# Sums of the normalised residual made one token tile at a time in a two-layer trunk kernel, and one sum for the down product made one place earlier

## What is computed

```python
def reference(x, norm_mix, w_in, sinks, w_s, b_s, w_o, norm_ffn, w_up, w_down, norm_final):
    for l in range(DEPTH):                      # DEPTH = 2
        h = rms_norm(x, norm_mix[l])
        proj = h @ w_in[l]
        ...                                     # att: windowed attention, sgu: spatial gating
        x = x + jnp.concatenate([att, sgu], axis=-1) @ w_o[l]
        h = rms_norm(x, norm_ffn[l])
        x = x + jnp.square(jax.nn.relu(h @ w_up[l])) @ w_down[l]
    return rms_norm(x, norm_final)
```

## Time and profile before

| | us |
|---|---|
| timed runs (3) | 948.45, 950.86, 953.03 |
| median | 950.86 |
| profiled execution: its own time | 949.33 |
| profiled execution: span of the trace | 947.4 |
| TensorE busy in the span | 930.3 (98%) |
| VectorE busy | 707.8 (75%) |
| ScalarE busy | 563.8 (60%) |
| GpSimd busy | 204.8 (22%) |
| mean granted TensorE clock, share of full speed | 0.994 |

### The profile page before, as it was taken

How to read it: one execution, slowest core, us unless ns; L and a number is a source line. 1 busy time by engine, 2 the same in 40 slices (tenths; PEclk the granted TensorE clock), 3 DMA queues, 4 the chain that set the end, 5 groups by cost and what they waited for, 6 DMA issues and landing times.

```text
span 947.4 us, 14055 instructions
## 1 busy us (share of the span) xinstructions
PE 930.3 (98%) x5632; PEld 819.0 (86%) x5632; DVE 707.8 (75%) x813; ACT 563.8 (60%) x843; POOL 204.8 (22%) x136
## 2 busy tenths in 40 slices
PE   8999999989999999999999999999899999999997
PEld 5888889978998998899888887899689989989985
DVE  5685525999779869879948752478987897798697
ACT  5556517775576376457655574377645756754764
POOL 2554224110011101011146433240101101101010
PEclk9999999999999999999999999999999999999999
DMA  9442150677668676676543320518668666676772
GB/s 292 127 135 71 42 150 28 167 166 206 147 171 204 134 232 134 178 190 156 165 150 134 112 68 23 155 24 245 139 173 205 149 198 158 161 198 150 205 156 89
DMA packets 40497, 141.76 MB, mean 150 GB/s; under 512 B 5616, under 2 KB 5744, under 8 KB 40432
## 3 DMA queue, kind: packets, MB, share of 16 engines
q1 hardware_dynamic: 28624, 98.32, 30.9%
q0 software_dynamic: 11520, 41.95, 25.3%
q10 hardware_dynamic: 288, 0.59, 0.2%
HBM read 138.74 MB, written 2.10 MB: 149 GB/s over the span
## 4 chain that ended last, share of the span: by engine, by line
PE 89%; DVE 6%; DMA 2%; ACT 1%; issue 1%; POOL 0%; DVEq 0%
PE bank L578 15%; PE bank L579 14%; PE bank L580 14%; PE bank L581 13%; PE bank L583 13%; PE bank L582 13%; DVE wlo L1316 2%; DMA raw<-weights_in 2%; PE bank L605 1%; PE bank L833 1%; PE bank L781 1%; DVE raw L1593 1%; PE bank L816 1%; PE bank L826 1%; PE bank L807 1%
## 5 line engine op out<-in xcount | busy, mean ns | idle before, releaser
L938 ACT ACTIVATE whi<-raw 128x1024 fp32r<-128x1024 f32 x268 | 281.0, 1057 | 165.2 <-PE bank L580 81.2
L1316 DVE TENSOR_TENSOR wlo<-raw,whi 128x1024 fp32r<-128x1024 f32 x218 | 264.8, 1223 | 79.8 <-ACT whi L938 79.4
L581 PE MATMUL bank<-xhi,wlo 128*128 128x256 f32 (+1 forms) x672 | 208.8, 311 | 0.0
L583 PE MATMUL bank<-xlo,whi 128*128 128x256 f32 (+1 forms) x672 | 207.3, 309 | 0.0
L582 PE MATMUL bank<-xhi,whi 128*128 128x256 f32 (+1 forms) x672 | 207.2, 308 | 0.0
L578 PE MATMUL bank<-wlo,fhi 128*128 128x512 f32 x448 | 176.3, 393 | 7.8 <-DVE flo L1580 7.8
L550 POOL DMA_DIRECT2D raw<-weights_in x80 | 69.4, 868 | 509.8 <-DVE raw L1593 236.0
L537 POOL TENSOR_TENSOR wlo<-raw,whi 128x1024 fp32r<-128x1024 f32 x50 | 135.2, 2714 | 195.4 <-ACT whi L938 195.4
L579 PE MATMUL bank<-whi,fhi 128*128 128x512 f32 x448 | 175.8, 392 | 0.0
L580 PE MATMUL bank<-whi,flo 128*128 128x512 f32 x448 | 175.5, 392 | 0.0
L581 PEld LDWEIGHTS bank<-xhi,wlo 128*128 128x128 f32 x672 | 128.3, 191 | 6.8 <-issue 0.3
(11 more groups left out here) (131 smaller groups left out, 1240.7 us busy)
## 6 DMA issues: line engine op xcount, KB each, us to landing
raw<-weights_in SPq DMA_DIRECT2D x172, 512.0 KB, 4.3
raw<-weights_in POOLq DMA_DIRECT2D x80, 512.0 KB, 6.1
xt<-x_in SPq DMA_DIRECT2D x4, 512.0 KB, 8.3
gbc<-gains_in SPq DMA_DIRECT2D x4, 512.0 KB, 4.3
out_t<-xt SPq DMA_DIRECT2D x3, 512.0 KB, 2.6
gbc<-gains_in ACTq DMA_DIRECT2D x1, 512.0 KB, 5.8
bias<-alibi_in SPq DMA_DIRECT2D x2, 256.0 KB, 7.3
wst<-ws_in SPq DMA_DIRECT2D x2, 256.0 KB, 7.0
```

The source lines that it names most:

```text
L581: pe.matmul(o, wlo[:, s, wc], hi[:, tokens], start=first, stop=False, skip_group_check=on_sum)
L583: return pe.matmul(o, whi[:, s, wc], lo[:, tokens], start=False, stop=last, skip_group_check=on_sum)
L938: act.activation(whi[:, n % SLOTS, :], raw_at(slot), ACT.Copy).then_inc(whi_ready, 1)
L1316: dve.tensor_tensor(wlo[:, n % SLOTS, :], raw_at(raw_slot(n)), whi[:, n % SLOTS, :], ALU.subtract) \
```

## The change

The four sums of the normalised residual are each made in two halves of 128 x 4 x 128, by tile pair. `made_x` counts the halves. The first half of S3 now stands between `turned_low` of tile 2 and `normed` of tile 3; the first halves of the other three stand between `normed` of tile 3 and `turned_low` of tile 3. The second halves stand where the whole sums stood. ScalarE waits for the second half of each. In the first quarter only, `make(q, 0)` moves ahead of the second low part of down's M1. The bodies of the sums are the same but for the token range.

```diff
+def made_x(l, i, k):
+    return l * 8 + 4 * k + i + 1
...
-                    made, src = ((1, s3), (3, xf[:, 0, :, :]), (2, xf[:, 3, :, :]), (4, xf[:, 1, :, :]))[i]
-                    act.wait_ge(xs_made, l * 4 + made)
+                    made, src = ((0, s3), (2, xf[:, 0, :, :]), (1, xf[:, 3, :, :]), (3, xf[:, 1, :, :]))[i]
+                    act.wait_ge(xs_made, made_x(l, made, 1))
...
+                def xs_make(i, k):
+                    x11, x12, x22, x21 = (xf[:, b, :, tok(k)] for b in range(4))
+                    if i == 0:
+                        dve.wait_ge(xf_ready, l * 2 * NT + 6 + 2 * k)
+                        dve.tensor_tensor(s3[:, :, tok(k)], x11, x21, ALU.subtract).then_inc(xs_made, 1)
+                    elif i == 1:
+                        dve.wait_ge(xs_made, made_x(l, 0, k))
+                        dve.tensor_tensor(x21, x22, x21, ALU.subtract).then_inc(xs_made, 1)
+                    elif i == 2:
+                        dve.wait_ge(xs_made, made_x(l, 1, k))
+                        dve.scalar_tensor_tensor(x11, x21, -1.0, x11, ALU.mult, ALU.subtract).then_inc(xs_made, 1)
+                    else:
+                        dve.wait_ge(xs_made, made_x(l, 2, k))
+                        dve.scalar_tensor_tensor(x12, x11, -1.0, x12, ALU.mult, ALU.subtract).then_inc(xs_made, 1)
...
                 for t in range(NT):
                     add(1, t)
                     if t:
                         turned_low(2 * l + 1, t - 1)
+                    if t == NT - 1:
+                        xs_make(0, 0)
                     normed(2 * l + 1, t)
+                for i in range(1, 4):
+                    xs_make(i, 0)
                 turned_low(2 * l + 1, NT - 1)
...
-                        xs_make(0)
+                        xs_make(0, 1)
                         low_up(q, M7, 0)
...
                         low_down(q, M1, 0)
+                        make(q, 0)
                         low_down(q, M1, 1)
                     else:
...
                         up_sum(q, M5, 1)
-                    make(q, 0)
+                        make(q, 0)
                     low_down(q, M7, 0)
```

More of the change, by code:

```diff
@@ L1626, in _ @@
                         low_up(q, M7, 1)
-                        xs_make(1)
-                        xs_make(2)
+                        xs_make(1, 1)
+                        xs_make(2, 1)
                         low_up(q, M6, 0)
@@ L1640, in _ @@
                         low_up(q, M5, 0)
-                        xs_make(3)
+                        xs_make(3, 1)
                         up_sum(q, M4, 0)
```

## The result

| | median, us | range, us | runs | profiled execution: own time, span |
|---|---|---|---|---|
| before | 951.23 | 948.45 to 953.03 | 7 | 949.33, 947.4 |
| after | 957.86 | 954.78 to 959.74 | 7 | 959.74, 957.9 |

The ratio of after to before is 1.0069 with a 95% interval of 1.0048 to 1.0089: the changed kernel is slower by 0.7%. That is 3.5 us above the forecast of 954.4, and 0.36 us outside the range.

A forecast was written before the change was run, and what follows sets the result against it. TensorE, busy 98%, was taken as the bound, with 11.2 us to win at its waits. 949.33 + 6.0 of new waits - 2.4 won = 952.9, plus 1.5 to the median: 954.4 us; 8-in-10 range 947.5 to 957.5.

The forecast's parts named there:

- The mechanism and place of the loss: Tile 3's norm: half sum and scaling wait for GpSimd on the shared SBUF port; TensorE waits 3.0 us a layer.
- that rival: Tile 3's norm: VectorE starts ahead of GpSimd; 951.7 us for both layers, about 953 for one; chance 0.25.
- The rival that the ports don't matter: Tile 3's norm: no turns with GpSimd, TensorE waits 2.4 us less; 948.5, or 945.1 with clock up; chance 0.18.
- The head start: VectorE behind tile 3: the first three halved sums save about 0.54 us each there, 1.6 us together.
- The gain ahead of M6: Down's first quarter: S3 fills VectorE's hole before M1's second low part; 2.4 us won in both layers.
- the upper end: Down's M1: its second weight block lands earlier, so the whole hole is won, 0.94 and 1.49 us.
- The lower end of the prediction: Down's M1: the block lands no earlier and ScalarE holds M7's low part; only 0.18 us won in layer 0.
- The argument on the queues: Ahead of M1's load: sums come 1.6 us earlier, accumulating transfers too, so queues are less full and the block lands earlier.
- Two falls in four places: TensorE's waits at M6 and tile 3's transposes, both layers: the clock falls twice, as many as before.
- The prediction's own figure for four falls: 957.8 us if the clock falls behind all four waits, at 1.7 us a fall.
- The slower rival: The clock falls behind the norm's new waits too, four falls at 1.7 us: 957 to 960 us; chance 0.12.

The follow-up runs named there:

- halves_only: The changed kernel with down's S3 back in its old place, so only the halved sums: 956.89 us, 1.0068 to before.
- psum_input: The changed kernel, but the half sum ahead of tile 3's scaling reads one input from PSUM instead of its SBUF copy: 951.16 us, 1.0009 to before.
- vector_first: The changed kernel, but GpSimd starts the low part of up's M2, second block, only after tile 3's scaling: 953.21 us, 1.0025 to before.
- halves_behind: The changed kernel with all four first half sums behind tile 3's scaling: 952.99 us, 1.002 to before.
- small_adds: Before with down's S3 moved and the first quarter's accumulating transfers for down's M7 cut to 64 of 1024 columns: 946.73 us, 0.996 to before.
- s3_turn: Before with down's S3 moved; first quarter's second accumulating transfer for down's M7 issued only after M1's second block landed: 947.83 us, 0.9956 to before.
- s3_only: The kernel before with only the move of down's S3 ahead of M1's second low part, first quarter: 951.68 us, 1.0005 to before.
- s3_turn_hidden: The kernel of `s3_turn` with ScalarE making M5's first hidden half ahead of the high part of M1's second block: 947.4 us, 0.995 to before.

## Why the prediction was right and wrong

**The mechanism and place of the loss: right.** The first half sum was forecast at 1.6 us and took 1.63 and 1.61. GpSimd was to be ahead by 0.04 and 0.02 us and was, by 0.05 and 0.01. The scaling was forecast at 3.5 (3.39 and 3.42), TensorE's waits at 3.0 (2.74 and 2.73). `halves_only` carries the whole loss; `psum_input` shows that the two inputs in SBUF are its condition; and `vector_first`, built so that VectorE wins the race, lands at 953.21 where that rival put 951.7 for both layers: its 1.6 us of waits came (1.3), but nothing was given back ahead of M6. The rival that the ports don't matter is out.

**The head start: right that it is small, and smaller still.** Where the half sums cost least (`halves_behind`), no gain from them is to be seen.

**The gain ahead of M6: wrong.** The step that failed is "I take the upper end: 0.94 + 1.49 = 2.4 us won". The block landed no earlier. ScalarE in after, layer 0:

```profile
200.27 1.06 ACT L943 ACTIVATE whi<-raw 128x1024 fp32r<-128x1024 f32 x1 [2.22 <-DMA raw<-weights_in]
```

It waited 2.22 us, against 2.17 in before, and it started 4.3 us later in time, as VectorE's run here did (199.16 for 194.90). The lower end of the prediction is what came, by the mechanism that it named for it. VectorE in after, layer 0:

```profile
199.16 1.22 DVE L1321 TENSOR_TENSOR wlo<-raw,whi 128x1024 fp32r<-128x1024 f32 x1
200.30 1.22 DVE L1571 TENSOR_TENSOR s<-hid,a 128x1024 f32<-128x1024 f32 x1
201.43 1.22 DVE L1321 TENSOR_TENSOR wlo<-raw,whi 128x1024 fp32r<-128x1024 f32 x1
203.50 1.22 DVE L1321 TENSOR_TENSOR wlo<-raw,whi 128x1024 fp32r<-128x1024 f32 x1 [0.85 <-ACT whi L943]
...
215.29 1.22 DVE L1589 TENSOR_TENSOR flo<-hid,fhi 128x1024 fp32r<-128x1024 f32 x1
```

The hole of 0.94 us went from M1's low part to M7's, one instruction on, and the run from the first to the last line took 16.13 us against 16.22. Of the 2.4 us the list of waits shows 0.5, and that is the wait ahead of M7, which is gone in `halves_only` too. The argument on the queues followed the wrong transfer. GpSimd in after, with the accumulating transfers for up's M5 and down's M7:

```profile
176.51 0.86 POOL L555 DMA_DIRECT2D raw<-weights_in  x1 [5.07 <-DVE raw L1602]
...
189.05 0.86 POOL L555 DMA_DIRECT2D raw<-weights_in  x1 [11.68 <-DMA raw<-weights_in]
```

The one for up's M5 did come earlier: only 1.2 us later than 175.28, where ScalarE's copy at 174.21 came 4.3 later. The one for down's M7 did not: 4.1 later than 184.98. It waits for a plain load, and SyncE's plain loads came 4.3 us later as well (the second of this stretch at 182.69 for 178.42). It is the pair for down's M7 that keeps M1's block away, as `small_adds` and `s3_turn` show. An upper end taken for "earlier" should have asked which transfer is in the block's way.

The price named for the upper end was too high besides: with the block in time (`small_adds`) the waits shrank by 2.0 us and not 2.4.

**The clock: right in kind, wrong in number.** Two falls in four places were taken; the profiled execution had all four, one of them twice as long, and they cost 7.8 us where the sum held 3.4. The reason given was that 2.7 and 3.0 us are shorter than the waits of the earlier trace rows; that was no ground to leave two of them out. The prediction's own figure for four falls, 957.8 us, is the median to 0.1 us, but by chance: it holds 2.4 us of gain that did not come, and two falls more than before, where the median run had lost less to the clock than the profiled one.

**The sum, mended.** For the profiled execution: 949.33 + 5.5 - 0.5 + 4.4 + 1.1 = 959.8, measured 959.74; the forecast for it was 952.9 = 949.33 + 6.0 - 2.4. So the miss there is 1.9 us of gain, 4.4 of clock and 1.1 at the end of the program, less 0.5 on the new waits. On the medians it is 3.5 us: 1.9 of gain, less 0.5 on the new waits, and by difference some 2 for the clock and what else differs between executions.

**The slower rival was the case** in the profiled execution, with 0.12 of the chance; its range of 957 to 960 us holds the time and its place and condition were as told. That the median run had four falls too isn't shown, but `halves_only` had them at 957.14 us. The stated range ended at 957.5, inside that rival. Since the price of a fall was known and only its number was in doubt, in a kernel in which the new waits are nearly of the length of the old, the range should have reached over the whole of it.

**Left open.** The time and mean clock of one kernel differ from execution to execution, and no run was made that controls the falls. The postponed transfer wasn't tried with the sum in its old place. Nor was it tried to load M1's second block in another queue or from an earlier slot.

## What to carry to other kernels

An instruction of VectorE that reads two SBUF inputs isn't free in a gap of VectorE when GpSimd is at work: look up what GpSimd does there, count the wait and then who arrives first at the next turn, and if the gap must be used, give the instruction one input from PSUM. Filling a hole in an in-order engine moves it to the next instruction of the same releaser (0.94 us of hole here, 0.09 us won); it is worth filling only if the engine that releases the next instruction gets earlier too; follow the chain back (here VectorE, ScalarE, the transfer) before counting the hole as won. And where TensorE's waits cost clock as well, count each new wait of the length of the old ones with its fall, above all in the range.

## What the runs showed of the hardware

- The granted clock fell from its upper level to its lower also with waits of 2.7 to 2.9 us: with 2.74 and 2.73 us in after, and with 2.90 and 2.89 us in `small_adds`. In the earlier trace rows the shortest with a fall was 3.64. The length of the wait alone doesn't decide: in `s3_only` the clock stayed up behind 3.64 us ahead of M6 in layer 0 and fell behind 3.65 in layer 1, and in `s3_turn_hidden` it fell behind 3.08 us in layer 0 and not behind 2.89 in layer 1.
- A fall cost 1.7 us of TensorE's work (3.4 us at the lower level) in most places. In some it held twice as long: in after at M6 of layer 0 from 215.1 to 221.9, at a cost of 2.7 us, and in `small_adds` from 673.1 to 679.9, where the clock of the stretch 673 to 680 was 0.51.
- Runs of one kernel differ by up to 8 us, and the clock with them: `halves_only` took 952.61 us at a clock of 0.996 and 960.8 at 0.988. The one execution of after that was profiled was 1.9 us off the median.
- The same transfer landed at different times in two executions: ScalarE got M1's second block at 195.97 in before and at 197.32 in `s3_only`, though nothing in the order of transfers ahead of it was changed.
- A plain load is held up by accumulating transfers beside it: with 64 of 1024 columns in these, ScalarE's wait of 2.17 us was gone, and with the second of them postponed it was 1.53 us in layer 0 and gone in layer 1.
- GpSimd pays nothing when it is first: 2.35 us beside a waiting scaling, against 2.79 when it comes second and 2.42 for its low part before it.
